# Squaring and rounding the mlp's inner values on ScalarE instead of VectorE

## The reference, cut to what matters

```
def _sq_relu_mlp(hn, w1, w2):
    a = jax.nn.relu(hn @ w1)
    return (a * a) @ w2

for layer in range(DEPTH_2):          # DEPTH_2 = 2
    ...
    h = h + _sq_relu_mlp(_rmsnorm_2(h, norm_mlp[layer]), mlp_w1[layer], mlp_w2[layer])
```

## Time and profile before

| | |
|---|---|
| median of 3 runs | 2381.89 us (2379.78 to 2382.57) |
| profiled execution, its own time | 2381.79 us |
| its span in the trace | 2380.0 us |
| PE busy | 2340.3 us (98%) |
| DVE busy | 1690.5 us (71%) |
| ACT busy | 1338.0 us (56%) |
| granted PE clock | 0.999 over the span |
| mlp_in0 in the trace | about 1863 to 1958 us |
| mlp_in1 in the trace | about 2194 to 2284 us |

### The profile page before, as it was taken

The page is one execution under the profiler, slowest core; times in us unless marked ns, Lnnn a source line. Parts: engine busy times, 40 slices in busy tenths (PEclk is TensorE's granted clock), DMA queues, the critical chain, the costliest instruction groups (busy, mean ns, idle before and its releaser), DMA issues.

```text
span 2380.0 us, 55393 instructions
## 1 busy us (share of the span) xinstructions
PE 2340.3 (98%) x20003; PEld 2241.9 (94%) x20003; DVE 1690.5 (71%) x3317; ACT 1338.0 (56%) x2766; POOL 3.4 (0%) x9
## 2 busy tenths in 40 slices
PE   8999999999999999999999999999999999999998
PEld 8899999789999999999998999999899999988998
DVE  7667667877658787776677677657576785677875
ACT  5555556365556555565555565557755454466554
POOL 0000000000000000000000000000000000000000
PEclk9999999999999999999999999999999999999999
DMA  7535665335654444456655455654444555534664
GB/s 242 177 118 167 195 206 166 98 116 169 206 179 135 133 141 132 141 168 193 202 162 178 141 159 183 205 178 152 139 127 128 171 174 181 146 110 142 180 193 148
DMA packets 103408, 385.73 MB, mean 162 GB/s; under 512 B 11344, under 2 KB 13520, under 8 KB 103024
## 3 DMA queue, kind: packets, MB, share of 16 engines
q1 hardware_dynamic: 102784, 381.78, 51.9%
q0 software_dynamic: 496, 2.24, 0.3%
HBM read 382.93 MB, written 1.05 MB: 161 GB/s over the span
## 4 chain that ended last, share of the span: by engine, by line
PE 87%; DVE 7%; ACT 3%; issue 2%; DMA 0%; DVEq 0%; ACTq 0%; SPq 0%
PE acc L530 25%; PE acc L537 24%; PE acc L536 24%; DVE weights_lo L2152 2%; PE acc L748 1%; PE acc L750 1%; PE acc L749 1%; ACT weights_hi L1316 1%; PE acc L770 1%; PE acc L837 1%; DVE h L2311 1%; DVE y L2300 1%; PE acc L860 1%; PE acc L882 1%; PE acc L683 1%
## 5 line engine op out<-in xcount | busy, mean ns | idle before, releaser
L2152 DVE TENSOR_TENSOR weights_lo<-weights,weights_hi 128x512 fp32r<-128x512 f32 (+1 forms) x1160 | 753.6, 680 | 328.9 <-ACT weights_hi L1316 324.6
L1316 ACT ACTIVATE weights_hi<-weights 128x512 fp32r<-128x512 f32 (+1 forms) x1160 | 673.0, 618 | 184.2 <-PE acc L537 155.1
L530 PE MATMUL acc<-xn_parts,weights_hi 128*128 128x256 f32 (+1 forms) x2560 | 728.9, 285 | 9.3 <-DVE weights_lo L2152 7.2
L537 PE MATMUL acc<-xn_parts,weights_lo 128*128 128x256 f32 (+1 forms) x2560 | 717.4, 280 | 0.0
L536 PE MATMUL acc<-xn_parts,weights_hi 128*128 128x256 f32 (+1 forms) x2558 | 716.9, 280 | 0.0
L530 PEld LDWEIGHTS acc<-xn_parts,weights_hi 128*128 128x128 f32 x2560 | 482.3, 188 | 24.2 <-issue 11.9
L530 PE MATMUL acc<-arena_r,weights_hi 128*128 128x256 f32 (+1 forms) x1760 | 494.3, 281 | 3.0 <-DVE weights_lo L2152 1.6
L537 PE MATMUL acc<-arena_r,weights_lo 128*128 128x256 f32 (+1 forms) x1760 | 491.0, 279 | 0.0
L536 PE MATMUL acc<-arena_r,weights_hi 128*128 128x256 f32 (+1 forms) x1754 | 488.9, 279 | 0.0
L536 PEld LDWEIGHTS acc<-xn_parts,weights_hi 128*128 128x128 f32 x2558 | 482.4, 189 | 0.4
L537 PEld LDWEIGHTS acc<-xn_parts,weights_lo 128*128 128x128 f32 x2560 | 482.2, 188 | 0.0
(11 more groups left out here) (342 smaller groups left out, 2290.1 us busy)
## 6 DMA issues: line engine op xcount, KB each, us to landing
weights<-in_ffn_in SPq DMA_DIRECT2D x176, 512.0 KB, 4.0
weights<-in_ffn_out SPq DMA_DIRECT2D x64, 704.0 KB, 4.2
weights<-in_att_in SPq DMA_DIRECT2D x72, 512.0 KB, 3.6
weights<-in_mlp_in SPq DMA_DIRECT2D x64, 512.0 KB, 3.5
weights<-in_mlp_out SPq DMA_DIRECT2D x64, 512.0 KB, 3.7
weights<-in_ret_qk SPq DMA_DIRECT2D x32, 512.0 KB, 4.1
weights<-in_ret_v SPq DMA_DIRECT2D x32, 512.0 KB, 3.6
weights<-in_ret_g SPq DMA_DIRECT2D x32, 512.0 KB, 3.6
```

What stands on the lines that cost most here:

```text
L530: nc.tensor.matmul(acc, hi, src_hi, start=first, stop=False)
L537: return nc.tensor.matmul(acc, lo, src_hi, start=False, stop=last)
L1316: nc.scalar.activation(w_hi[phase.ring(sub)][:, 0:n, :], raw[slot][:, j * SUB:j * SUB + n, :], ACT.Copy)\
L2152: nc.vector.tensor_tensor(w_lo[phase.ring(sub)][:, 0:n, :], raw[slot][:, j * SUB:j * SUB + n, :], w_hi[phase.ring(sub)][:, 0:n, :].bitcast ...
```

## The change

ScalarE keeps relu and gets two more steps behind it: the square (L1967 in the changed kernel, from `silu` into `part`) and the rounding into `mlp_hi` (L1969). VectorE keeps the subtraction for `mlp_lo` (L2546). The semaphores keep their names and change hands: `part_ready` is now raised by ScalarE's square, `part_hi` by ScalarE's rounding. ScalarE waits for its own relu and for its own square, and, before it writes `part`, for the low half of the unit two before (`part_lo`). Relu no longer waits for `part_ready`. TensorE's instructions and the DMAs are the same.

```diff
@@ ScalarE, relu(phase, n)
                 def unit(i, u):
                     wait_unit(phase, i, u)
 
-                    act.wait_ge(part_ready, i * phase.body + (hidden0[phase.name] - DEPTH * FFN + u + 1))
+                    first, done = hidden0[phase.name], i * phase.body
                     nc.scalar.activation(silu[:, u % 2, 0:n], PS[:, u % SLOTS, 0:n], ACT.Relu).then_inc(out_evacuated, 1)
+                    act.wait_ge(out_evacuated, done + evacuated(phase, u + 1))
+                    act.wait_ge(part_lo, done + (first + u - 1))
+                    nc.scalar.activation(part[:, u % 2, 0:n], silu[:, u % 2, 0:n], ACT.Square).then_inc(part_ready, 1)
+                    act.wait_ge(part_ready, done + (first - DEPTH * FFN + u + 3))
+                    nc.scalar.activation(mlp_hi[:, :, :][:, bass.ds(done + u, 1), :].rearrange("p c t -> p (c t)")[:, 0:n],
+                                         part[:, u % 2, 0:n], ACT.Copy).then_inc(part_hi, 1)
                 stream(phase, unit)
@@ VectorE, square_relu(phase, n)
                 def unit(i, u):
-                    dve.wait_ge(out_evacuated, i * phase.body + evacuated(phase, u + 1))
-                    nc.vector.tensor_tensor(part[:, u % 2, 0:n], silu[:, u % 2, 0:n], silu[:, u % 2, 0:n], ALU.mult).then_inc(part_ready, 1)
-                    dve.wait_ge(part_ready, i * phase.body + (first - DEPTH * FFN + u + 3))
                     m = i * phase.body + u
-                    split_hidden(mlp_hi[:, m, 0:n], mlp_lo[:, m, 0:n], part[:, u % 2, 0:n], i * phase.body, u, first)
+                    dve.wait_ge(part_hi, m + (first + 1))
+                    nc.vector.tensor_tensor(mlp_lo[:, m, 0:n], part[:, u % 2, 0:n], mlp_hi[:, m, 0:n].bitcast(F32), ALU.subtract)\
+                        .then_inc(part_lo, 1)
                 stream(phase, unit)
```

## The result

The changed kernel takes 2391.3 us (median of 6 runs, 2386.9 to 2393.1), the one before 2381.9 (6 runs, 2379.3 to 2382.8): a ratio of 1.0038, 95% interval 1.0025 to 1.0051. Run again among the experiments it took 2388.9 us (6 runs) against 2381.4, ratio 1.0031 (1.0018 to 1.0043). The forecast was 2385.1 in a range of 2381 to 2390, "the same" with 0.66. The sign was right, the size was not: a loss of some 7 to 9 us instead of 3.3, and 2391.3 lies outside the range.

A forecast was written before the change was run, and what follows sets the result against it. TensorE, 98% busy, was taken to wait at unit boundaries for the weights' split. Loops 1.0 (mlp_in1) + 1.1 (mlp_in0), last units 0.3, phase ends 0.9 = +3.3 us on 2381.79: 2385.1 us, range 2381 to 2390.

The forecast's parts named there:

- The late starts at unit boundaries: TensorE's first matmul of a unit waits for the weights' split: 0.08 or 0.23 us late in mlp_in1 before.
- the chain from a unit's end to the split of the weights two units on: In mlp_in1, unit end through relu and split to first matmul: 2.64 or 2.79 us before, 2.79 after, allowance 2.56.
- ScalarE's part: Looped chain, 256 columns: relu 0.39, wait 0.10, square 0.41, wait 0.13, rounding 0.32, high part 0.62 us.
- The ends of the phases: Square and rounding delay Ln, Exp and mlp_out's second-unit weights behind the last relu; together +0.9 us.
- The branch's 0.09 falls on the chain that is not late and is covered: ScalarE's loop branch adds 0.09 us behind the rounding in one unit of four, but costs nothing.
- It just fits: VectorE's low half, with wait w = 0.20, clears before the weights' low part: 0.96 against 0.97 us after rounding starts.
- The 28 units of the loops: Late starts in the loop turns: +1.0 us in mlp_in1 and +1.1 in mlp_in0.
- the last four, written out: Last 4 units, own waits 0.03: 0.06 us late on two mlp_in1 starts, none in mlp_in0; +0.3 us.
- the low half in the way: Rival: VectorE's low half delays the weights' low part, from w = 0.21 on; +7.2 us, 2389.0; chance 0.31.
- that the own waits hide: Rival: register work runs ahead during relu and square, both ScalarE waits cost 0.03; 2380.5 us; chance 0.13.
- The ceiling: Removing all lateness in the mlp_in loop turns, 0.52 and 0.12 us a turn, gives at most 4.5 us.
- The +7 us that I had estimated from that figure: If semaphore reads lengthen ScalarE's two own waits by up to 0.07 us each, the chain grows 0.14.

The follow-up runs named there:

- low_behind: Changed kernel, but VectorE takes each inner low half one unit later, behind the weights' low parts, first loop turn written out on VectorE; ratio 1.0023.
- The three kernels at TensorE's own pace: ScalarE's square and rounding behind next weights; kernel before with VectorE's three steps behind them; kernel before with looped mlp_in units written out: 2376.4, 2376.2, 2375.9 us.
- the written-out kernel: Changed kernel with the 28 looped units of both mlp_in phases written out on ScalarE and VectorE; ratio 0.9999.
- after_scalar_written_out: Changed kernel with the looped mlp_in units written out on ScalarE alone; mlp_in1 93.98 us, mlp_in0 96.32, one execution.

## Why the prediction was partly right and its size wrong

**What held.** The late starts at unit boundaries, the chain from a unit's end to the split of the weights two units on, and that square and rounding stay in that chain when they change the engine. ScalarE's part was priced within hundredths: relu to square 0.49 (forecast 0.39 + 0.10), square to rounding 0.56 (0.41 + 0.13), rounding to high part 0.32, low part to matmul 0.74. The ends of the phases were forecast at +0.9 and are +0.43 and +0.59. After the last relu:

```profile
2288.30 0.38 ACT L1964 ACTIVATE silu<-acc 128x256 f32<-128x256 f32 x1 [0.67 <-PE acc L537]
2288.72 0.42 ACT L1967 ACTIVATE arena<-silu 128x256 f32<-128x256 f32 x1
2289.16 0.42 ACT L1969 ACTIVATE arena_r<-arena 128x256 fp32r<-128x256 f32 x1
2289.49 0.46 ACT L1502 ACTIVATE lnv<-acc,const_a 128x256 f32<-128x256 f32 x1
```

Ln starts 1.19 behind relu (forecast 1.18, before 0.43).

**The step that failed: "The branch's 0.09 falls on the chain that is not late and is covered", and "It just fits".** The 28 units of the loops were forecast at +2.1 us and are +5.8; the last four, written out, were forecast at +0.3 and are +0.65. low_behind parts the two failures. Its turns, with the low half out of the way, are 12.33 us in mlp_in0 and 11.75 in mlp_in1 (two of them 11.83), where 12.16 and 11.58 were forecast and the changed kernel has 12.41 and 11.95.

- *The branch on ScalarE*, 0.17 us a turn in each phase with what little the other terms were short. It was priced at 0.09 and put at nothing. From rounding to high part it takes 0.10 more than in the other units in mlp_in1 and 0.15 in mlp_in0, and it is not covered.
- *The low half on VectorE*, another 0.08 us a turn in mlp_in0 and 0.20 in mlp_in1. Its wait w was put at 0.20 and is 0.25 (rounding ends 2248.06 + 0.42 = 2248.48, low half 2248.73). The trace lists, for its line, 93 ns of address work and 40 ns of another register instruction. The point from which it decides was 0.21, so each chain is 0.04 longer.
- At the branch VectorE pays too, and the forecast's sum had no term for that. In mlp_in1 0.60 pass from the low half to the weights instead of 0.34. The chain of that unit is 0.04 + (2255.17 - 2252.85) + 0.74 = 3.10 us against 2.88 in the forecast's own terms.

Why the branch isn't covered: of two interlaced chains the late one is, in these traces, the one with the branch in it. Two units took 6.10 and 5.85 in mlp_in1, where I had 5.79 twice; in mlp_in0 6.13 (1886.81 to 1892.94) and 6.28 (to 1899.22), where I had 6.08 twice. Once settled that is 0.37 and 0.25 us more a turn; the first two turns of each phase together lose less.

**The rivals.** The first, the low half in the way, is real, and its price of +7.2 is near the measured +7.5 by luck: it gave the low half 3.9 us, and low_behind shows 2.0. The rest above the forecast is mostly the branch on ScalarE, which this rival did not have. It deserved more than 0.31, since I had left 0.01 us of room and one of the two register instructions unpriced. The second rival, that the own waits hide, is out: 0.11 and 0.13 from end to start, in the looped units.

**The ceiling.** I called 4.5 us the most these phases can give, since 0.52 and 0.12 us a turn were late. The three kernels at TensorE's own pace show 5.3: their turns take 10.88 and 11.84 us, where I had reckoned 10.92 and 11.88, and the last four units of mlp_in1 had 0.2 to give.

**The two rules of the Trainium skill.** ScalarE's square takes 0.42 us for 256 columns and VectorE's 0.42, so for the square alone the move is neutral in work, as forecast. The rounding is not: 0.29 us on VectorE (the CAST above), 0.42 on ScalarE. The Trainium skill (ScalarE: Activation LUTs, Rules for kernel authors) gives mul to VectorE as the faster engine; the trace doesn't show that for this square. The 50 to 100 ns for a sequencer's read of a semaphore (the Trainium skill, Advanced Engine Details and Errata, Network/Comms) are not what an own wait costs where the instruction carries it: 0.03 in the written-out kernel (2245.79 to 2245.82, 2246.24 to 2246.27). In the loop, with register instructions around it, it comes to 0.11 and 0.13. The +7 us that I had estimated from that figure is near the measured loss, but not by its mechanism, which would have lengthened each of ScalarE's two own waits by 0.07.

## What to carry to other kernels

When an engine that is half idle is offered work, don't ask how busy it is but what stands behind the new work in its queue. Here the weights of two units ahead did, and the same move cost 7.5 us with the new work in front of them and ended 5 us ahead of the old kernel with it behind them. Where one unit's work waits for the unit just multiplied, put it behind the next weights' split, not ahead: that removed every late start of the loops, on either engine. In a hardware loop a chain of dependent small instructions pays for register work at each wait and again at the branch; price both for each engine of the chain, and don't count on a neighbour to cover the longest chain of a turn.

## What the runs showed of the hardware

- A dependent step on one engine costs 0.03 us with constant targets. In the loops it costs 0.11 and 0.13 on ScalarE, and VectorE's wait for ScalarE costs 0.25 instead of 0.04. The square and the rounding on ScalarE take 0.42 us in both.
- A loop's branch costs 0.10 to 0.16 us between two instructions of an engine (ScalarE 0.42 instead of 0.32 in mlp_in1 and 0.49 instead of 0.34 in mlp_in0; VectorE 0.50 instead of 0.34). In mlp_in1 of the changed kernel it costs VectorE 0.26, and with turns of 8 units at most 0.07; the cause of that difference is open.
- In one execution (after_scalar_written_out) all of mlp_out1 ran slower: 100.03 us instead of 96.8, at a granted clock of 1.00, with matmul starts 0.118 us apart instead of 0.113 (40 of them in 4.71 against 4.53 us). The program's instructions of that phase are the same as in the changed kernel. It was seen in one execution, and its cause is open.
- Until mlp_in0, where all these kernels do the same work, executions differ by up to 4.2 us (1858.72 to 1862.87), which is the size of the effects at issue. Where it arises was not followed up.
